# Value products ahead of scores in an attention loop, a changed table of norms, and first products before a barrier

## The reference, cut to what matters

```python
h = rms_norm(x, attn_norm[l])
proj = h @ w_in[l]
# 6 forget-gate heads, 4 differential heads (two score maps each), 6 heads that attend to the 256 best keys
fq = rms_norm(fq...); fk = rms_norm(fk...)
dq = partial_rope(rms_norm(dq...)); dk = partial_rope(rms_norm(dk...))
sq = partial_rope(rms_norm(sq...)); sk = partial_rope(rms_norm(sk...))
o_fox = fox_attention(fq, fk, fv, cum_logf)      # softmax(q.k/sqrt(D) + c[t] - c[s]) v, causal
o_diff = diff_attention(dq, dk, dv, lam)         # (softmax - lam * softmax) v, causal
o_dsa = dsa_attention(sq, sk, sv, iq, ik, iw, 256)  # top-256 causal keys by an index score
x = x + jnp.concatenate([o_fox, o_diff, o_dsa], axis=-1) @ w_out[l]
h = rms_norm(x, ffn_norm[l])
gate, up = jnp.split(h @ w_gate_up[l], 2, axis=-1)
x = x + (jax.nn.silu(gate) * up) @ w_down[l]
```

## Time and profile before

| | us |
|---|---|
| Median of 3 runs | 2224.62 (2222.28 to 2230.28) |
| Profiled execution, its own time | 2226.6 |
| Its span | 2224.8 |
| PE busy | 2043.9 (92% of the span, 11592 instructions) |
| PE weight loads busy | 1749.1 (79%) |
| DVE busy | 1244.3 (56%) |
| ACT busy | 853.1 (38%) |
| POOL busy | 514.1 (23%) |
| Mean granted clock of PE | 0.957 |

### The profile page before, as it was taken

How to read it: one execution, slowest core, us unless ns; L and a number is a source line. 1 busy time by engine, 2 the same in 40 slices (tenths; PEclk the granted TensorE clock), 3 DMA queues, 4 the chain that set the end, 5 groups by cost and what they waited for, 6 DMA issues and landing times. The chain is left out here.

```text
span 2224.8 us, 30344 instructions
## 1 busy us (share of the span) xinstructions
PE 2043.9 (92%) x11592; PEld 1749.1 (79%) x11592; DVE 1244.3 (56%) x2346; ACT 853.1 (38%) x1402; POOL 514.1 (23%) x355
## 2 busy tenths in 40 slices
PE   6999998999999999899989999998899989799894
PEld 6898777788888888887778888877888878677673
DVE  3667765445344446776554444458942233488885
ACT  4444434322122345343342222123234452277772
POOL 2664312000000146433100000005355434200001
PEclk9999999999999999998999999999899999799997
DMA  4111100422231111111041331206546532589995
GB/s 158 58 58 39 48 20 20 180 114 77 93 113 57 43 58 58 39 39 32 36 178 59 113 113 70 100 1 182 86 116 194 174 123 98 210 334 405 399 370 209
DMA packets 61627, 270.95 MB, mean 122 GB/s; under 512 B 15040, under 2 KB 19904, under 8 KB 37056
## 3 DMA queue, kind: packets, MB, share of 16 engines
q1 hardware_dynamic: 52864, 237.84, 30.5%
q10 hardware_dynamic: 6048, 22.02, 2.6%
q0 software_dynamic: 2592, 9.44, 1.2%
HBM read 244.14 MB, written 37.19 MB: 126 GB/s over the span
## 5 line engine op out<-in xcount | busy, mean ns | idle before, releaser
L1253 PE MATMUL fill_ps<-w_hi,h_hi 128*128 128x256 f32 (+1 forms) x704 | 212.8, 302 | 13.9 <-ACT values L872 5.1
L1253 PE MATMUL fill_ps<-w_hi,h_lo 128*128 128x256 f32 (+1 forms) x704 | 204.0, 290 | 0.0
L1253 PE MATMUL fill_ps<-w_lo,h_hi 128*128 128x256 f32 (+1 forms) x704 | 203.8, 289 | 0.0
L516 DVE TENSOR_TENSOR ffn_silu<-ffn_silu,ffn_up 128x512 f32<-128x512 f32 x44 | 30.2, 687 | 285.7 <-ACT ffn_silu L474 285.7
L322 POOL TENSOR_SCALAR norm_ss<-norm_ss 128x1 f32<-128x1 f32 x24 | 4.8, 201 | 799.6 <-ACT ffn_raw_d L316 739.4
L801 POOL TENSOR_TENSOR w_lo<-w_raw,w_hi 128x1024 fp32r<-128x1024 f32 x60 | 150.3, 2517 | 150.2 <-ACT w_hi L864 150.2
L1253 PEld LDWEIGHTS fill_ps<-w_hi,h_hi 128*128 128x128 f32 x704 | 140.3, 199 | 26.2 <-issue 14.9
L528 DVE TENSOR_TENSOR x<-ffn_down,x 128x512 f32<-128x512 f32 x176 | 119.1, 689 | 71.3 <-PE ffn_down L590 70.4
L1719 POOL TENSOR_TENSOR w_lo<-w_raw,w_hi 128x1024 fp32r<-128x1024 f32 x48 | 126.1, 2641 | 131.1 <-ACT w_hi L1826 131.1
L474 ACT ACTIVATE ffn_silu<-ffn_up 128x512 f32<-128x512 f32 x44 | 26.3, 598 | 336.3 <-PE ffn_up L575 336.2
L575 PE MATMUL ffn_up<-h_hi,w_hi 128*128 128x512 f32 x384 | 151.9, 395 | 3.3 <-PEq L778 3.3
(11 more groups left out here) (456 smaller groups left out, 5551.8 us busy)
## 6 DMA issues: line engine op xcount, KB each, us to landing
moe_raw_gu<-in_w_e_gu SPq DMA_DIRECT2D x46, 1024.0 KB, 11.4
w_raw<-in_w_mix SPq DMA_DIRECT2D x28, 1024.0 KB, 5.0
w_raw<-in_w_two SPq DMA_DIRECT2D x23, 1024.0 KB, 5.0
moe_raw_d<-in_w_e_down SPq DMA_DIRECT2D x23, 1024.0 KB, 8.4
w_raw<-in_w_gate SPq DMA_DIRECT2D x22, 1024.0 KB, 5.9
w_raw<-in_w_up SPq DMA_DIRECT2D x22, 1024.0 KB, 6.7
ffn_raw_d<-in_w_down SPq DMA_DIRECT2D x22, 1024.0 KB, 4.9
moe_in<-in_zero SPq DMA_DIRECT2D x23, 512.0 KB, 7.7
```

What stands on the lines that cost most here:

```text
L516: nc.vector.tensor_tensor(act_t[:, b, :], act_t[:, b, :], up_ps[1][b][:], ALU.mult).then_inc(prod_done, 1)
L1253: last = nc.tensor.matmul(b[:, 0:cols], aw[:, k, t * P:(t + 1) * P], ww[:, k, 0:cols], start=k == 0 and n == 0, stop=k == KD - 1 and n == 2)
```

## The change

Five things change; the second block's own work stays, but for its first two products.

1. In each attention step PE does the value product of step n-3 right behind the transposes, ahead of the scores and the filler.
2. The first 36 dense parts of the loop are spread at 2.4 a step instead of 2, the rest from step 15 instead of 18; dense work ends with step 41 instead of 44. Output products keep their steps.
3. The norms of groups 3 to 7 have steps of their own table, mostly one to four steps earlier, with a free step between the sum and the scaling; the scaling of group 5, formerly in one piece, is done in two. The steps of the search fill what the norms leave free.
4. `EarlyProducts`: at each seam the first products of the next stage are issued between the norm's last transposes, ahead of the barrier. From the start to the first mixer, and from feed-forward 0 to mixer 1, these are all of dense chunk 0 (96 matmuls of 256 columns); from a mixer to its feed-forward, and from feed-forward 1 to the second block, half of the tokens of two products (48 matmuls of 256 columns), the other half following behind the barrier. All PSUM banks are now shared (`core.banks`), so that these products can be left in a bank across the barrier.
5. At the start, the constants are loaded in two pieces, the first weights right after the second tile of x, and they are split between the tiles' norms.

The diff, cut to its core:

```diff
+class EarlyProducts:
+    def tokens(self, pe, t):
+        h, ww = (self.core.h_hi, self.core.h_lo), (self.core.w_hi[0], self.core.w_lo[0])
+        pe.wait_ge(self.done, 2 * t + 2)
+        for k in range(KD):
+            for n, (x, y) in enumerate(((0, 0), (1, 0), (0, 1))):
+                self.core.nc.tensor.matmul(self.core.banks[t][:, 0:MIX_WIDTH], h[x][:, k, t * P:(t + 1) * P],
+                                           ww[y][:, k * MIX_WIDTH:(k + 1) * MIX_WIDTH], start=k == 0 and n == 0, stop=k == KD - 1 and n == 2)
+    def features(self, pe, bank, s, f, k0, k1, half):
...
-    DENSE.setdefault(_n // 2 if _n < 36 else 18 + (_n - 36) * 3 // 4, []).append(_x)
+    DENSE.setdefault(_n * 5 // 12 if _n < 36 else 15 + (_n - 36) * 3 // 4, []).append(_x)
...
-SQUARE_AT = {0: 3, 11: 4, 17: 5, 35: 6, 44: 7}
+SQUARE_AT = {0: 3, 9: 4, 14: 5, 32: 6, 41: 7}
...
+for _p, _steps in ((3, (1, 3, 4)), (4, (10, 12, 13, 14, 15)), (5, (15, 17, 18, 19, 20)), (6, (33, 35, 36, 37, 38)), (7, (42, 44, 45, 46, 48))):
+    for _n, _x in zip(_steps, ("sum", (0, 1), (2, 3), "gain", "turn")):
+        NORM_AT.setdefault(_n, []).append((_p, _x))
...
                     if 2 <= n < STEPS + 2:
                         turn_probs(n - 2)
+                    if 3 <= n < STEPS + 3:
+                        value(n - 3)
                     if n < STEPS:
                         score(n)
...
-                    if 3 <= n < STEPS + 3:
-                        value(n - 3)
-                for t in range(1, TB):
-                    norm.turn(pe, t)
+                norm.turn(pe, 1)
+                norm.turn(pe, 2)
+                pe.wait_ge(lo_done, split(MIX_CHUNKS, 1))
+                early.features(pe, core.banks[4], gate, 0, 0, KD // 2, 0)
+                norm.turn(pe, 3)
+                early.features(pe, core.banks[4], gate, 0, KD // 2, KD, 0)
+                early.features(pe, core.banks[5], gate, 1, 0, KD, 0)
...
-                down(groups - 1, (groups - 1) % 2, {NT - 3: (0,), NT - 1: (1, 2, 3)})
+                down(groups - 1, (groups - 1) % 2, True)
+                norm.turn(pe, 1)
...
+                if next_tokens:
+                    early.tokens(pe, 0)
+                    norm.turn(pe, 2)
+                    early.tokens(pe, 1)
+                    norm.turn(pe, 3)
+                    early.tokens(pe, 2)
+                    early.tokens(pe, 3)
```

More of the change, by code:

```diff
@@ L293, in split_lo, with __init__ @@
                                           ALU.subtract).then_inc(self.lo_done, 1)
+class EarlyProducts:
+    def __init__(self, core, done):
+        self.core, self.done = core, done
+    def tokens(self, pe, t):
[6 more added lines that the diff above has]
+    def features(self, pe, bank, s, f, k0, k1, half):
+        h, ww = (self.core.h_hi, self.core.h_lo), (self.core.w_hi[s], self.core.w_lo[s])
+        if half == 0:
+            pe.wait_ge(self.done, TB)
+        cols = slice(half * SEQ // 2, (half + 1) * SEQ // 2)
+        for k in range(k0, k1):
+            at = k * 2 * P + f * P
+            for n, (x, y) in enumerate(((0, 0), (1, 0), (0, 1))):
+                last = self.core.nc.tensor.matmul(bank[:, cols], ww[y][:, at:at + P], h[x][:, k, cols],
+                                                  start=k == 0 and n == 0, stop=k == KD - 1 and n == 2)
+        return last
 class NextNorm:
@@ L433, in feed_forward @@
         first = FirstChunks(core, f"{name}_next", next_chunk, st)
+        early = EarlyProducts(core, norm.lo_done)
         with nc.Block() as block:
@@ L593, in down @@
                         last.then_inc(down_sum, 1)
-                        for t in turns.get(n, ()):
-                            norm.turn(pe, t)
+                        if last_group and n == NT - 3:
+                            norm.turn(pe, 0)
                 def step(g, s, first):
@@ L697, in mixer @@
         sub = [core.sb(f"subln_ss{m}", [P, TB * 2], ctx=st) for m in range(2)]
[L698 to L701, removed]
+        s_ps, t_ps, o_ps, fill = core.banks[0:3], core.banks[3:5], core.banks[5][:, 0:TB * HEAD], core.banks[6:8]
         o = o_flat[:].rearrange("p (t d) -> p t d", t=TB)
@@ L734, in mixer @@
         out_summed, added, chain = sem("out_summed"), sem("added"), sem("chain")
-        order = [("dense", n) for n in range(3 * TB)] + [("idx", n) for n in range(3)]
+        order = [("dense", n) for n in range(TB, 3 * TB)] + [("idx", n) for n in range(3)]
         order += [("dense", n) for n in range(3 * TB, 5 * TB - 1)] + [("unit", 0), ("unit", 1), ("dense", 5 * TB - 1), ("unit", 2), ("unit", 3)]
@@ L746, in bank @@
         def bank(kind, i):
+            if kind == "dense" and i < TB:
+                return core.banks[i]
             return fill[place[kind, i] % 2]
@@ L1359, in out @@
                     last.then_inc(out_summed, 1)
-                for c in range(3):
+                for c in range(1, 3):
                     for t in range(TB):
@@ L1498, in second_mixer @@
         w_moe = ExpertWeights(core, w, last)
-        banks = [core.psum(f"bank2_{b}", [P, SEQ], st) for b in range(8)]
+        banks = core.banks
+        early = EarlyProducts(core, None)
         fill, s_ps, t_ps, o_ps = banks[0:2], banks[2:5], banks[5:7], banks[7]
@@ L2449, in turn_at @@
                     last.then_inc(at_turned, 1)
-                for f in range(SQT):
+                for f in range(2):
+                    claim("u", f)
+                    early.features(pe, bank("u", f), 0, f, 0, KD, 1).then_inc(summed, 1)
+                for f in range(2, SQT):
                     features("u", f, f // 2, (f % 2) * P, (h_hi, h_lo), KD, 0, KD)
@@ L3095, in build @@
         core.raw = [core.sb(f"w_raw{s}", [P, KD * MIX_WIDTH], ctx=pers) for s in range(2)]
+        core.banks = [core.psum(f"bank{b}", [P, SEQ], pers) for b in range(8)]
         load_and_norm(core, w)
@@ L3113, in load_and_norm @@
         gain_row = core.sb("n1_gain_row", [P, D], ctx=st)
-        norm = NextNorm(core, "n1", [s[:] for s in slots], gain_row[:], [core.psum(f"n1_ps{b}", [P, SEQ], st) for b in range(4)], st)
+        norm = NextNorm(core, "n1", [s[:] for s in slots], gain_row[:], core.banks[4:8], st)
         first = FirstChunks(core, "start", lambda c: w["w_mix"][0, c], st)
+        early = EarlyProducts(core, norm.lo_done)
         x_dram = w["x"].rearrange("a (t p) d -> p (a t) d", p=P)
@@ L3158, in _ @@
                 pe.wait_ge(const_in, 16)
-                for t in range(TB):
-                    norm.turn(pe, t)
+                norm.turn(pe, 0)
+                norm.turn(pe, 1)
+                pe.wait_ge(first.lo_done, 1)
+                early.tokens(pe, 0)
+                norm.turn(pe, 2)
+                early.tokens(pe, 1)
+                norm.turn(pe, 3)
+                early.tokens(pe, 2)
+                early.tokens(pe, 3)
 def constants():
```

58 lines of the change are left out of this document (37 added, 21 removed).

## The result

The changed kernel takes 2274.07 us in the median (2269.45 to 2277.75), the kernel before 2226.2 (2222.28 to 2230.28): a ratio of 1.0214, 95% interval 1.0185 to 1.0242. It is slower by 48 us, where 2229 us, about no change, was forecast: outside the stated range of 2202 to 2254.

What follows compares the result with a forecast made beforehand. The loop was held to be bound by turns by PE and the scores-DVE-store chain. Per layer 9.3 + 14.8 - 14.0 - 1.9 = +8.2, both +16.4, less 12.4 at boundaries: +4.0, giving 2229 us; range 2202 to 2254.

Steps and rivals of the forecast that it cites:

- Part 1: Attention loop: each head's first value product waits for DVE's store, costing 9.3 us (light half) plus 14.8 (first half) per layer.
- Part 2: Attention loop: the new norm table removes PE's waits behind late norms, 14.0 us per layer, though part may stay.
- Part 3: Attention loop clock: two half-clock stretches, 10 us lost instead of 11.9, so 1.9 us gained per layer.
- Rival B: Attention loop: recurring waits lower the clock repeatedly, six stretches, 30 us lost instead of 11.9; 2256 us, chance 0.19.
- Part 4: Five stage boundaries: products of the next stage done while PE waits between norm transposes, 12.4 us gained (6 to 15).
- The two from mixer to feed-forward: Mixer-to-feed-forward boundaries: 48 matmuls going ahead gain 4.2 us each (2.5 to 4.8), taken from a working of 4.6.
- The two of dense chunk 0: Start and feed-forward 0 to mixer 1: chunk 0 done early gains 4.2 us and 2.5 us.
- the sign for it: Mixer 1: dense chunk 1 would start 2.5 to 3.4 us sooner after the last feed-forward product.
- The second block's 2.7 us of later DVE work: Feed-forward 1 to second block: early products delay the barrier and DVE's first work, a loss of 2.7 us (0 to 3.5).

Runs made afterwards that it cites:

- the tables alone: The kernel before with only the new tables of dense parts, norms and search; value products last, seams as before: 2189.93 us, ratio 0.9855.

## Why the prediction was wrong

- **Part 1, the waits: right.** Forecast 24.1 us per layer in 16 places, measured 22.8 in 16. The light half's seven waits are 0.89 to 1.16 us, 7.3 us in all instead of 9.3, because addition and store overlap a little on DVE (342.50 to 343.73 is 1.23 us, where I had 1.36) and the transposes take 0.38 us, where I had 0.31; the nine of the first half came to 15.5 against 14.8, the first 2.39 instead of 1.35. That the two sums came out so close is partly luck: single ones were off by up to 1.0 us either way, and 0.12 + 0.70 + 0.77 - 0.31 is 1.28, not 1.2. That these waits are paid in full, with nothing to hide them, was right too.
- **Part 2, the waits removed: right in its sum, by luck in part.** PE's other waits fell from 16.0 to 1.9 us, 14.1 against the 14.0 forecast. But 5.6 of the 14.0 were value waits, and those of the changed kernel are all counted in Part 1. With the tables alone PE's idle time falls by 9.8 us in each loop: 1.0 of the 5.6 goes, 4.5 stays, while the dense wait of 2.1 us that I left standing goes as well. What stays is nearly the 5.6 us that I had priced, but not taken, for DVE's operations beside POOL's splits. The earlier trace rows show that case only in part: their DVE scaling starts ahead of the split, but behind another subtraction of POOL's, at 157.05 and 1.29 us long. What was missed besides is what goes with the waits when no new wait takes their place: with the tables alone the clock stays up as well, 10.2 and 3.4 us per layer, which the changed kernel never saw.
- **Part 3, the clock: the step that failed.** I took two stretches at half clock per layer and 10 us lost to them, 1.9 gained; there are 9 and 11, and 27.3 and 37.5 us lost, 15.4 and 25.6 more than before. It failed in its reading of the earlier trace rows: falls had come behind pairs of waits, and a single one of 2.1 us had brought none, so I called single waits safe. That was one case taken for a rule, and the second pair was misread. In the kernel before:

```profile
268.07 0.41 PE L1333 MATMUL o_ps<-values,prob_t 128*128 128x64 f32 x2 [2.85 <-issue]
271.50 0.79 PE L1357 MATMUL fill_ps<-w_hi,h_hi 128*128 128x512 f32 x1 [1.62 <-DVE x L1223]
```

```profile
268.07:269.80 1.73, 1.73 (x12) 1.33 (x12) 1.73 (x5) 0.00 (x0) 1.44 (x1) 1.00 0.05 9
269.80:271.50 1.70, 0.08 (x2) 0.00 (x1) 1.66 (x6) 0.62 (x2) 0.00 (x0) 0.51 0.42 87
```

PE was busy from 268.07 to 269.88, when the second wait began; the clock had fallen at 269.83, behind the single wait of 2.85 us. So the trace of the kernel before already spoke against the rule, though other single waits there, of 2.1 and 2.4 us, brought no fall. In the changed kernel single waits of 1.16 us bring the clock down and others of the same length don't; 7 and 10 of the 16 per layer had a fall in them or close behind. Rival B had the mechanism and the sign. It still was too small, by 18 us: it took six stretches where 9 and 11 came, and let half-clock matmuls hide 6 us of waits. Its chance of 0.19 was too low for a term whose ends lay 30 us per layer apart.
- **Part 4, the seams: a sum not far off, from terms partly wrong.** 12.4 forecast, 8 to 10 measured alone. The two from mixer to feed-forward gain 4.2 us each; that this is the forecast's digit is luck, since its working gave 4.6. The two of dense chunk 0 gain nothing (6.7 forecast). Chunk 1 of mixer 1 does begin 3.5 us sooner, as the sign for it said (2.5 to 3.4), but I took 0.9 us for the cold start, and of the 3.5 us only 1.0 is left at its last matmul. The second block's 2.7 us of later DVE work is there; whether it is paid at the end, no run shows.

In the Trainium skill, page "TensorE: Matmul & The Clock Gate", the section "A second HAM failure mode: psum-queue depth-cycling" tells of a clock that goes up and down over many short idle times. The filled waits bear it out for this kernel: 64.8 us were lost at half clock in both loops with the waits left empty (27.3 and 37.5), 10.2 with ten transposes in each (3.4 and 6.8).

## What to carry to other kernels

A product moved ahead of other work on an engine takes its waits along: before moving it, look at what it waits for, and at all that stands ahead of that on the other engine. Where the wait is for a buffer to be emptied, look first whether a second buffer can be had, which here turned a loss of 2% into a gain of 2%; 1.5% of that gain is there without moving the products at all, from the tables and seams. And cost a wait on PE not at its length alone: against the version with the products put back, the sixteen waits per layer cost 36 us in idle time and 54 us in slower products, both layers together.

## What the runs showed of the hardware

PE's clock fell behind single waits of 1.16 us in a loop that otherwise kept PE busy, and did not fall behind others of the same length (366.62 and 343.83 us). Useless transposes of a constant in such a wait kept it up: 2 and 3 falls per loop instead of 9 and 11, and 36 us less, though they added 23.8 us of PE work to each loop. A DVE product of two SBUF tiles, 128x512, took 0.69 us by itself and 2.37 us beside a subtraction on POOL (170.25 and 171.66 us, tables alone).
